# Delta-net inverse on one core: D made as a transpose of the updated E and copied by ScalarE, with the fills and VectorE's side work in another order

## The reference

```
kk = jnp.where(strict, jnp.einsum('bhncd,bhnmd->bhncm', kb, k) * decay, 0.0)
rhs = jnp.concatenate([v * beta[..., None], kb * jnp.exp(gc)[..., None]], axis=-1)
sol = lax.linalg.triangular_solve(kk + eye, rhs, left_side=True, lower=True, unit_diagonal=True)
u, w = sol[..., :dv], sol[..., dv:]
```

## Time and profile before

| | |
|---|---|
| time, median of 3 runs | 3576.83 us (3576.43 to 3578.93) |
| span of the profiled execution | 3576.0 us |
| PE busy | 3237.9 us, 91% of the span |
| DVE (VectorE) busy | 1219.7 us, 34% |
| ACT (ScalarE) busy | 465.5 us, 13% |
| delta-net stage, PE work of heads 0 to 7 | about 134.5 us to 692 us of the span |

### The profile page before, as it was taken

How to read it: one execution, slowest core, us unless ns; L and a number is a source line. 1 busy time by engine, 2 the same in 40 slices (tenths; PEclk the granted TensorE clock), 3 DMA queues, 4 the chain that set the end, 5 groups by cost and what they waited for, 6 DMA issues and landing times.

```text
span 3576.0 us, 23142 instructions
## 1 busy us (share of the span) xinstructions
PE 3237.9 (91%) x9516; PEld 1650.4 (46%) x9516; DVE 1219.7 (34%) x2121; ACT 465.5 (13%) x811; POOL 139.3 (4%) x118
## 2 busy tenths in 40 slices
PE   3998999889998989999889998979766899999999
PEld 3566666634444434444334444434333455444444
DVE  2554555324432021011124442030287653233310
ACT  0212111110000011111010000021222232100000
POOL 0000000000000010000000000000132000000000
PEclk9998999799998999999999999989866776999999
DMA  6011111114342211111113432111100200112111
GB/s 257 32 61 81 48 48 56 63 49 162 144 158 85 83 71 71 71 50 74 47 47 149 157 144 102 72 58 76 71 0 0 94 1 1 47 73 91 56 65 56
DMA packets 23448, 274.54 MB, mean 77 GB/s; under 512 B 3368, under 2 KB 4264, under 8 KB 5936
## 3 DMA queue, kind: packets, MB, share of 16 engines
q1 hardware_dynamic: 19296, 264.35, 19.5%
q10 hardware_dynamic: 4048, 8.73, 0.7%
HBM read 270.97 MB, written 2.10 MB: 76 GB/s over the span
## 4 chain that ended last, share of the span: by engine, by line
PE 45%; DVE 5%; ACT 1%; issue 1%; POOL 0%; DVEq 0%; ACTq 0%
PE bank L288 17%; PE bank L246 13%; PE bank L1026 3%; PE bank L1418 2%; PE bank L1433 2%; PE bank L1447 1%; DVE arena L1253 1%; PE bank L1163 1%; PE bank L1040 1%; PE bank L1033 1%; PE bank L237 1%; DVE arena L1521 0%; PE bank L1047 0%; PE bank L234 0%; DVE arena L1195 0%
## 5 line engine op out<-in xcount | busy, mean ns | idle before, releaser
L288 PE MATMUL bank<-HT,ring 128*128 128x512 f32 x2112 | 918.8, 597 | 24.8 <-ACT HT L357 18.4
L246 PE MATMUL bank<-arena,ring 128*128 128x512 f32 x1440 | 634.9, 601 | 17.7 <-issue 16.3
L288 PEld LDWEIGHTS bank<-HT,ring 128*128 128x128 f32 x2112 | 402.4, 191 | 526.7 <-issue 523.1
L246 PEld LDWEIGHTS bank<-arena,ring 128*128 128x128 f32 x1440 | 277.7, 193 | 369.0 <-issue 367.5
L311 DVE SCALAR_TENSOR_TENSOR XT<-bank,mod,XT 128x512 f32<-128x512 f32 x48 | 36.1, 751 | 702.5 <-PE bank L246 702.5
L487 PE MATMUL bank<-HT,ring 128*128 128x512 f32 x512 | 250.7, 620 | 0.0
L402 DVE TENSOR_SCALAR arena<-bank,ffc 128x512 f32<-128x512 f32 x88 | 65.9, 748 | 521.2 <-PE bank L288 521.2
L215 DVE SCALAR_TENSOR_TENSOR arena<-ring,evec,arena 128x512 f32<-128x512 f32 x252 | 189.0, 750 | 7.0
L441 ACT ACTIVATE arena<-arena,ffc 128x512 f32<-128x512 f32 x66 | 47.7, 722 | 831.4 <-DVE arena L405 831.4
L405 DVE SCALAR_TENSOR_TENSOR arena<-bank,ffc,arena 128x511 f32<-128x511 f32 (+1 forms) x176 | 131.9, 749 | 6.2
L487 PEld LDWEIGHTS bank<-HT,ring 128*128 128x128 f32 x512 | 92.9, 199 | 77.3 <-issue 77.3
(11 more groups left out here) (339 smaller groups left out, 3142.6 us busy)
## 6 DMA issues: line engine op xcount, KB each, us to landing
ring<-w_ada SPq DMA_DIRECT2D x36, 2048.0 KB, 8.1
ring<-w_up SPq DMA_DIRECT2D x33, 2048.0 KB, 8.1
ring<-w_down SPq DMA_DIRECT2D x24, 1408.0 KB, 5.9
ring<-w_gdn SPq DMA_DIRECT2D x8, 2048.0 KB, 12.4
ring<-w_ret_qk SPq DMA_DIRECT2D x4, 2048.0 KB, 8.0
ring<-w_ret_v SPq DMA_DIRECT2D x4, 2048.0 KB, 8.1
ring<-w_ret_g SPq DMA_DIRECT2D x4, 2048.0 KB, 8.2
ring<-w_ret_out SPq DMA_DIRECT2D x4, 2048.0 KB, 8.0
```

Source lines behind the costliest of these rows:

```text
L246: last = nc.tensor.matmul(bank[:, :], w[:, n % per_load, k, :], src(k), start=(k == 0), stop=(k == kc - 1))
L288: last = nc.tensor.matmul(B[2 * (j % 2) + half][:, :], w[:, 2 * (j % 2) + half, k, :], HT[:, k, :], start=(k == 0), stop=(k == KC - 1))
```

## The change

In the levels l = 1 to 5 the group of matmuls DT = D Tm is gone, and so is VectorE's subtraction that updated D. In their place PE transposes the updated E (four transposes against the identity, into bank 6), and ScalarE copies the bank into D. PE therefore waits, inside a level, for VectorE's update of E, and at the start of the levels 2 to 6 for ScalarE's copy. The second fill is cut in two: one of its two matmuls stands ahead of the transposes, the other behind them. On VectorE the ada step moves from between Tm and the updates to behind the update of E, and of the two convolution taps one moves ahead of the update of E. The number of fill matmuls, ada steps and taps stays the same. No DMA is added, removed or moved.

```diff
@@ pe_gdn
-                def fill(part):
+                def fill(part, n0=0, n1=2):
                     if h + 1 < GH:
-                        pe_dense4(pe, ("gdn", h + 1), 2 * part, 2 * part + 2)
+                        pe_dense4(pe, ("gdn", h + 1), 2 * part + n0, 2 * part + n1)
...
                 for l in range(1, 7):
-                    pe.wait_ge(dve_done, at("dve", "gdn", "D", h, l - 1))
                     if l == 1:
+                        pe.wait_ge(dve_done, at("dve", "gdn", "D", h, 0))
                         pe.wait_ge(act_done, at("act", "gdn", "LT", h))
+                    else:
+                        pe.wait_ge(act_done, at("act", "gdn", "D", h, l - 1))
                     for i in range(NT):
                         last = nc.tensor.matmul(B4[5][:, i, :], G["LT4"][:, i, :], G["D4"][:, i, :], start=True, stop=True)
                     last.then_inc(pe_done, PE.tick("gdn", "LD", h, l))
                     fill(2 * l + 1)
                     pe.wait_ge(dve_done, at("dve", "gdn", "Tm", h, l))
                     pe.wait_ge(dve_done, at("dve", "gdn", "inv", h, l - 1))
-                    if l < 6:
-                        for i in range(NT):
-                            last = nc.tensor.matmul(B4[6][:, i, :], G["E4"][:, i, :], G["Tm4"][:, i, :], start=True, stop=True)
-                        last.then_inc(pe_done, PE.tick("gdn", "DT", h, l))
                     for i in range(NT):
                         last = nc.tensor.matmul(B4[4][:, i, :], G["Tm4"][:, i, :], G["E4"][:, i, :], start=True, stop=True)
                     last.then_inc(pe_done, PE.tick("gdn", "TE", h, l))
                     if l < 6:
-                        fill(2 * l + 2)
+                        fill(2 * l + 2, 0, 1)
+                        pe.wait_ge(dve_done, at("dve", "gdn", "inv", h, l))
+                        for i in range(NT):
+                            last = nc.tensor.transpose(B4[6][:, i, :], G["E4"][:, i, :], ident[:, :])
+                        last.then_inc(pe_done, PE.tick("gdn", "ET", h, l))
+                        fill(2 * l + 2, 1, 2)
@@ act_gdn, after the copy of LT
+                for l in range(1, 6):
+                    act.wait_ge(pe_done, at("pe", "gdn", "ET", h, l))
+                    nc.scalar.activation(G["D"], B[6][:, :], ACT.Copy).then_inc(act_done, AC.tick("gdn", "D", h, l))
@@ dve_gdn
                     nc.vector.tensor_tensor(G["Tm4"], B4[5], level(maskL, l), ALU.mult).then_inc(dve_done, DV.tick("gdn", "Tm", h, l))
-                    dve_ada(dve, 0, 4 + h, l - 1, l)
-                    if l < 6:
-                        dve.wait_ge(pe_done, at("pe", "gdn", "DT", h, l))
-                        nc.vector.tensor_tensor(G["D"], G["D"], B[6][:, :], ALU.subtract).then_inc(dve_done, DV.tick("gdn", "D", h, l))
+                    if h + 1 < GH:
+                        dve_conv4(dve, h + 1, (l - 1) // 2, 2 * ((l - 1) % 2), 2 * ((l - 1) % 2) + 1)
                     dve.wait_ge(pe_done, at("pe", "gdn", "TE", h, l))
                     nc.vector.tensor_tensor(G["E"], G["E"], B[4][:, :], ALU.subtract).then_inc(dve_done, DV.tick("gdn", "inv", h, l))
+                    dve_ada(dve, 0, 4 + h, l - 1, l)
                     if h + 1 < GH:
-                        dve_conv4(dve, h + 1, (l - 1) // 2, 2 * ((l - 1) % 2), 2 * ((l - 1) % 2) + 2)
+                        dve_conv4(dve, h + 1, (l - 1) // 2, 2 * ((l - 1) % 2) + 1, 2 * ((l - 1) % 2) + 2)
```

## The result

The changed kernel takes 3595.73 us in the median of four runs (3591.11 to 3598.97), before 3577.08 us in the same comparison. The ratio is 1.0049, with a 95% interval of 1.0035 to 1.0063: 18.7 us slower. Five more runs of it, on another occasion, gave 3598.0 us and 1.0053 [1.0040, 1.0067]. The profiled execution took 3593.14 us, with a span of 3591.3, so the profile has 15.3 of the 18.7 us.

The account below looks back on a forecast made before the run. PE was taken to bound levels with fills, and the serial chain of PE and VectorE head 7. Gaining 5.3 us and losing 20 gave +14.7 on 3576.8, about 3591 us, range 3577 to 3600.

Parts of the forecast that it names:

- Levels with fills: Heads 0 to 6, levels 1 to 5: DT's 0.89 us replaced by 0.44 of transposes, net gain 0.15 us after waits.
- Two waits: Filled level: PE waits 0.20 us for E's update before the transposes and 0.10 for ScalarE's copy before LD.
- 35 levels, 5.3 us: Heads 0 to 6, five levels each: the 0.15 us gained per level adds up to 5.3 us.
- the shift of the clock's fall and rise at the borders: Borders between heads: low clock may move, half a microsecond a head either way, 3.5 us; taken as nothing.
- Head 7, low clock: Head 7's levels, without fills: serial chain at half clock, 7.56 us a level, 17.7 us more; 20 us with later stages.
- U, W and the start of the scan: Head 7 behind its levels: low clock adds 1.8 us in U and W and some 0.5 in the scan's first steps.
- Why the clock stays low: Head 7: a low level has 16 entries in 6 us, a full one 23, against 35 that kept full clock before.
- rival 1: Head 7: full clock returns from level 2, levels of 5.27 us, 6.7 us more; 3578 us in all, chance 0.17.
- Transposes do not count: Head 7: if transposes do not engage the full clock, only 16 of a level's 20 entries count, making 20 us surer.
- The moved tap, ScalarE's queue, SyncE's queue: Filled levels: tap ends 0.15 us before TE's result, ScalarE idle at the copies, SyncE's order kept; no cost taken.
- The whole: Whole kernel: 5.3 us gained in heads 0 to 6, 20 lost in head 7, +14.7, about 3591 us; chance 0.62.

Follow-up runs that it names:

- the runs with 2 and 0: Changed kernel, head 7 in the old scheme, with both second-fill matmuls (2) or none (0) ahead of the transposes: 3602.24 and 3600.91 us.
- measured with the clock held: Changed kernel plus unread matmuls at the head borders and four in the gap ahead of head 7's levels: 3553.28 us, ratio 0.9932.

## Why the prediction was right, and where it was not

The forecast was 3591 us, slower, within 3577 to 3600; the measured 3595.73 and 3598.0 lie in it. The mechanism was the one forecast: the shorter levels bring little, and head 7's serial chain at the low clock brings the loss. Some of the nearness of the number is luck, as the last point says.

- *Levels with fills.* Two waits of 0.20 and 0.10 us were taken; the level came out at 5.89 us and not 5.96, 0.22 us gained in place of 0.15. Late weights cost the transposes some 0.06 us (317.35 to 317.85, against 0.44 covered) and not the 0.11 taken from a group of matmuls. That the two cut fills cover just the two waits is shown by the runs with 2 and 0, at 6.61 and 6.66.
- *35 levels, 5.3 us.* The sum over levels was the step that failed. They save 7.7 us of PE's work, and 2.1 us came out in the run with heads 0 to 6 alone (the interval reaches from -5.4 to +1.1 us); in the two profiles of the changed kernel head 7 begins 2.2 us sooner than before and at the same time as before. I had set the shift of the clock's fall and rise at the borders to nothing, with 3.5 us either way. It is not a chance term: from the third border on every head gave the gain back, with a low stretch of 17.0 us in place of 13.6 and the head's length unchanged at 71.7, while the two heads ahead of that, with 13.6, had 70.6 and 71.1. In heads without a low stretch the 1.1 us is there, 67.9 to 66.8. Why both schemes settle at the same 71.7 us is not shown.
- *Head 7, low clock.* Levels of 7.52 us against 7.56, 17.2 us lost against 17.7; U, W and the start of the scan 2.3, as taken. Within the full kernel this was right to 3%, 19.5 us for 20 in both profiles. With the new scheme in head 7 alone the levels lost 17.5 us and the run only 13.6: how soon the clock comes back behind the levels was no term of the sum.
- *Why the clock stays low.* The time was right, the reason half. I had argued from the density of entries that a level in the new scheme could neither bring the clock back nor keep it. The first holds. The second does not: 20 entries in 5.22 us at 1.00 kept it for 30 us. What decides is the clock at which level 1 begins, and so the idle 3.4 us ahead of it, which are the same in both kernels; before, the clock came back in the denser levels, in the sparser ones it does not.
- *Full clock in head 7* (rival 1) was priced at 5.27 us a level and 6.7 us in all against a head 7 that begins low; measured with the clock held, 5.22 us and 6.7 us over the old scheme. The two 6.7 are different sums (the measured one is five levels of 1.34 us more), so that they agree to the digit is chance.
- *Transposes do not count.* The Trainium skill, "TensorE: Matmul & The Clock Gate", Part 4, states this beside durations for bf16. The runs do not bear it out for fp32 where the clock is to be held: 32 transposes with no matmul among them kept the granted clock at 1.00 across a gap at whose end it fell to 0.50 without them. Whether transposes alone bring it up from 0.50, no run shows.
- *The moved tap, ScalarE's queue, SyncE's queue.* As taken, nothing: E's update starts 1.10 us after TE in the level shown, an odd one, with the tap that waits for the projection ahead of it.
- *The whole* came out 5 to 7 us above 3591. In the first profile, heads 0 to 6 gave 2.2 us in place of 5.3, head 7 cost 19.5, and the stages behind gave back 2.0, which the sum had at nothing: 15.3 against the 14.7 forecast. In the second, heads 0 to 6 gave nothing, head 7 cost 19.5, and the stages behind 1.3 more: 20.8. The first comes so near through an error and a chance gain that offset each other.

The fastest version is neither kernel: the new scheme where fills cover its waits, the old one in head 7, and matmuls nobody reads in PE's idle stretches, 3546.62 us, 0.85% under before and 49 us under the changed kernel. That the new scheme has a part in it is not shown: the old one with the same matmuls has 3551.98 us, the two intervals overlap, and heads 0 to 6 take as long in both.

## What to carry to other kernels

Replacing PE work by a hop over two more engines shortens a step only where independent work covers both hops (5.89 us for 6.11, against 7.5 or 5.2 for 3.9 uncovered); keep the old form in the last iteration, which has no next one to borrow from. A shorter step need not give a shorter run: here 1.1 us a head were saved and hardly any of it arrived. When a shorter step does not shorten the iteration, compare the granted clock's low stretches, in length and in what they fall on, before looking for a new wait. An idle gap ahead of a sparse serial stretch cost that stretch half its clock here; a few useless matmuls in the gap are the cheapest thing to try.

## What the runs showed of the hardware that was not expected

- The same entries of PE, levels 1 to 6 of head 7, run steadily at either clock: 43.0 us at 0.50 when PE had been idle for 3.4 us ahead of them, 30.0 us at 1.00 when it had not.
- fp32 transposes against the identity hold a granted clock of 1.00 as matmuls do (over 4.0 us with little else, then over 33.4 us with both).
- Heads with a low stretch at their border settle at 71.7 us in both schemes, though the levels differ by 1.1 us: low 13.6 us in one case, 17.0 in the other.
- Useless PE work made the kernel 26 us faster (3551.98 for 3578.15), but two more of the same matmuls per border took 5 us of it away again.
